# Compressed keys of all heads as one item of attention, and a round in the order transpositions, projection pieces, scores, values

## The reference

```python
def hybrid_mixer(h, cos, sin, w_in, cmp_pos, cmp_w1, cmp_w2, w_branch_nsa, w_branch_dil, w_out):
    q_n, kv_n, g_n, qkv_d, g_m = jnp.split(h @ w_in, cuts, axis=-1)
    ...
    kc = compress(kv_n[:, :, 0], cmp_pos[0], cmp_w1[0], cmp_w2[0])
    vc = compress(kv_n[:, :, 1], cmp_pos[1], cmp_w1[1], cmp_w2[1])
    ...
    y_nsa = nsa_attention(q_n, q_r, kc, vc, ks, kv_n[:, :, 3], kw, kv_n[:, :, 5], gates)
    ...
    y_dil = jnp.sum(alpha[..., None] * jnp.stack(outs, axis=2), axis=2).reshape(B, T, DIL_W)
    merged = g_m[:, :, 0] * (y_nsa @ w_branch_nsa) + g_m[:, :, 1] * (y_dil @ w_branch_dil)
    return merged @ w_out
```

## Time and profile before

| | |
|---|---|
| median of 3 runs | 1186.07 us (1183.7 to 1187.54) |
| the profiled execution | 1184.49 us |
| its span | 1182.7 us, mean TensorE clock 0.996 |
| busy, share of the span | TensorE 99%, VectorE 47%, ScalarE 34%, GpSimd 14% |
| the mixer | about 385 to 823 us |
| its attention stage | about 434 to 670 us |

### The profile page before, as it was taken

How to read it: one execution, slowest core, us unless ns; L and a number is a source line. 1 busy time by engine, 2 the same in 40 slices (tenths; PEclk the granted TensorE clock), 3 DMA queues, 4 the chain that set the end, 5 groups by cost and what they waited for, 6 DMA issues and landing times.

```text
span 1182.7 us, 16772 instructions
## 1 busy us (share of the span) xinstructions
PE 1170.4 (99%) x6707; PEld 956.4 (81%) x6707; DVE 561.5 (47%) x855; ACT 400.8 (34%) x532; POOL 170.3 (14%) x196
## 2 busy tenths in 40 slices
PE   9999999999999999999999999999999999999997
PEld 6888888888888987877777888888888888888886
DVE  6444344463333557567666444643544434432222
ACT  6323323232223225443535522233332332322222
POOL 1000000000112481356662000021000000000000
PEclk9999999999999999999999999999999999999998
DMA  7332333223336831412331233332333233223321
GB/s 228 107 105 75 104 106 90 76 73 99 97 97 153 189 81 46 95 46 43 79 79 31 73 98 89 107 107 71 107 106 105 76 103 106 82 77 98 98 74 71
DMA packets 211299, 110.85 MB, mean 94 GB/s; under 512 B 32112, under 2 KB 207648, under 8 KB 211248
## 3 DMA queue, kind: packets, MB, share of 16 engines
q1 hardware_dynamic: 206832, 104.97, 33.3%
q0 software_dynamic: 4256, 5.02, 1.7%
q10 hardware_dynamic: 160, 0.14, 0.0%
HBM read 105.06 MB, written 2.10 MB: 91 GB/s over the span
## 4 chain that ended last, share of the span: by engine, by line
PE 98%; DVE 1%; DMA 0%; SPq 0%; ACT 0%; issue 0%; DVEq 0%; ACTq 0%
PE ps L1300 23%; PE ps L1301 22%; PE ps L1302 22%; PE ps L1419 7%; PE ps L1418 7%; PE ps L1417 7%; PE ps L1558 2%; PE ps L1491 2%; PE ps L1535 2%; PE ps L1508 1%; PE ps L1574 1%; PE ps L1530 1%; DMA x_nat<-in_x 0%; PE ps L1478 0%; PE ps L1549 0%; PE ps L1524 0%
## 5 line engine op out<-in xcount | busy, mean ns | idle before, releaser
L930 DVE TENSOR_TENSOR w_lo<-w_raw,w_hi 128x2048 fp32r<-128x2048 f32 (+5 forms) x116 | 224.5, 1935 | 380.5 <-ACT w_hi L693 380.3
L1300 PE MATMUL ps<-xg_hi,w_hi 128*128 128x512 f32 x992 | 390.6, 394 | 0.4 <-DVE xg_lo L1212 0.4
L1302 PE MATMUL ps<-xg_hi,w_lo 128*128 128x512 f32 x992 | 386.4, 390 | 0.0
L1301 PE MATMUL ps<-xg_lo,w_hi 128*128 128x512 f32 x992 | 386.2, 389 | 0.0
L693 ACT ACTIVATE w_hi<-w_raw 128x2048 fp32r<-128x2048 f32 (+3 forms) x104 | 180.5, 1736 | 337.5 <-PE ps L1302 214.9
L1300 PEld LDWEIGHTS ps<-xg_hi,w_hi 128*128 128x128 f32 x992 | 186.2, 188 | 43.8 <-issue 6.2
L1302 PEld LDWEIGHTS ps<-xg_hi,w_lo 128*128 128x128 f32 x992 | 186.2, 188 | 39.2
L1301 PEld LDWEIGHTS ps<-xg_lo,w_hi 128*128 128x128 f32 x992 | 186.3, 188 | 37.2
L1417 PE MATMUL ps<-p_hi,w_hi 128*128 128x512 f32 x352 | 137.0, 389 | 0.0
L1419 PE MATMUL ps<-p_hi,w_lo 128*128 128x512 f32 x352 | 136.9, 389 | 0.0
L1418 PE MATMUL ps<-p_lo,w_hi 128*128 128x512 f32 x352 | 136.9, 389 | 0.0
(11 more groups left out here) (198 smaller groups left out, 1159.3 us busy)
## 6 DMA issues: line engine op xcount, KB each, us to landing
w_raw<-in_ffn_w_in SPq DMA_DIRECT2D x86, 512.0 KB, 5.0
w_raw<-in_w_in SPq DMA_DIRECT2D x32, 512.0 KB, 5.2
w_raw<-in_ffn_w_out SPq DMA_DIRECT2D x32, 384.0 KB, 3.6
w_raw<-in_ffn_w_out SPq DMA_DIRECT2D x32, 320.0 KB, 4.1
w_raw<-in_w_in SPq DMA_DIRECT2D x24, 256.0 KB, 4.6
w_raw<-in_w_out SPq DMA_DIRECT2D x8, 512.0 KB, 4.0
x_nat<-in_x SPq DMA_DIRECT2D x8, 256.0 KB, 4.9
w_raw<-in_w_branch_nsa SPq DMA_DIRECT2D x8, 256.0 KB, 4.1
```

The lines of the kernel that those rows point to most:

```text
L930: lo = V.tensor_tensor(w_lo[:, s, c], w_raw[:, s, c], w_hi[:, s, c].bitcast(F32), ALU.subtract)
L1300: mm(out, ah, bh, start=(first and i == 0), stop=False)
L1301: mm(out, ah, bl, start=False, stop=False)
L1302: last = mm(out, al, bh, start=False, stop=(final and i == len(pairs) - 1))
```

## The change

The item "cmp" is done once for all heads. The four heads' scores over 32 keys now stand side by side and fill the 128 columns of each query tile; softmax, transposition and copy are done on all of it. VectorE's and ScalarE's instructions of that item are four times as wide, TensorE transposes 8 blocks of 128 columns instead of 8 of 32 in each of four items, and the transposed probabilities go into a buffer of their own, `cmp_probs_t` (the tile `square`, free by then). The value products of head hh are issued at the head of its first "nsa" item (pe_cmp_values); for hh = 0 in the item's own place, at index 4 of the list. The compressed values are computed into four row groups for that. There are 25 NSA items and 41 in all, and 40 fills in rounds -1 to 38.

The scores, masks and exponentials of items 0 and 1 move ahead of the stage, before the first half of chunk 12 and before the second. The rounds change on all three engines.

```diff
         for hh in range(HPG):
-            ITEMS.append(("cmp", hh))
             ITEMS += [("nsa", hh, i, qts) for qts in ((0, 1), (2,), (3,)) for i in range(2)]
+        ITEMS.insert(4, ("cmp", 0))
...
-                                         ("hidden_t",), ("chunk", N_CH1, (0, KD // 2)), ("cmp_kv",),
-                                         ("chunk", N_CH1, (KD // 2, KD)), ("read_rest",), ("attend", 0, len(ITEMS))]
+                                         ("hidden_t",), ("scores", 0), ("chunk", N_CH1, (0, KD // 2)), ("cmp_kv",),
+                                         ("scores", 1), ("chunk", N_CH1, (KD // 2, KD)), ("read_rest",), ("attend", 0, len(ITEMS))]
...
         def act_attend(act, a, b):
-            act_exp(act, a)
-            act_exp(act, a + 1)
             for n in range(a, b):
                 act_copy_probs(act, n)
-                if n + 2 < b:
-                    act_exp(act, n + 2)
-                if n > a and ends_pair(n - 1) is not None:
-                    act_y(act, n - 1)
                 c = filled(n - 1)
                 if c is not None and ends_unit(c):
                     act_split(act, MIX0 + CH[c][1] + 2)
                 if splits_y(n) is not None:
                     act_split_y(act, splits_y(n))
+                if n + 2 < b:
+                    act_exp(act, n + 2)
+                if n > a and ends_pair(n - 1) is not None:
+                    act_y(act, n - 1)
...
                 if n + 1 < b:
                     dve_factor(dve, n + 1)
-                if n + 2 < b:
-                    dve_prepare(dve, n + 2)
-
                 for unit, half in SPLITS.get(n, ()):
                     dve_split(dve, MIX0 + unit, half=half)
                 if splits_y(n - 1) is not None:
                     dve_split_y(dve, splits_y(n - 1))
+                if n + 2 < b:
+                    dve_prepare(dve, n + 2)
...
             if it[0] == "cmp":
-                hh = it[1]
                 for g in range(2):
-                    mm(ps[:, b + g, :].rearrange("p (q k) -> p q k", q=TT)[:, :, 0:NC], ident_b,
-                       cmp_b.rearrange("p (q n) -> p q n", q=TT), start=True, stop=False)
+                    mm(ps[:, b + g, :].rearrange("p (q h n) -> p q h n", q=TT, h=HPG), ident_b,
+                       cmp_b.rearrange("p (q n) -> p q n", q=TT).unsqueeze(2).broadcast_to([P, TT, HPG, NC]),
+                       start=True, stop=False)
                 for qt in range(TT):
-                    for g in range(2):
-                        rows = slice(g * DH, g * DH + DH)
-                        last = mm(ps[:, b + g, qt * P:qt * P + NC], pool[rows, Q_RAW + hh, qt * P:qt * P + P],
-                                  k_cmp[rows, 0:NC], start=False, stop=(qt == TT - 1))
+                    for hh in range(HPG):
+                        for g in range(2):
+                            rows = slice(g * DH, g * DH + DH)
+                            at = qt * P + hh * NC
+                            last = mm(ps[:, b + g, at:at + NC], pool[rows, Q_RAW + hh, qt * P:qt * P + P],
+                                      k_cmp[rows, 0:NC], start=False, stop=(at == T - NC))
...
+        def pe_cmp_values(hh, opens):
+            rows = slice(hh * NC, hh * NC + NC)
+            for at, w in ((0, T),) if opens else ((0, 3 * P), (3 * P, P)):
+                for g in range(2):
+                    last = mm(ps[g * DH:g * DH + DH, 6, at:at + w], v_cmp[rows, g, :],
+                              cmp_probs_t[rows, g * T + at:g * T + at + w], start=opens, stop=False)
+            return last
...
         def pe_attend(pe, a, b):
-            pe_scores(pe, a)
-            pe_scores(pe, a + 1)
             pe_fill(pe, -1)
             for n in range(a, b):
                 pe_transpose_probs(pe, n)
+                if n in FILL:
+                    pe_fill(pe, n)
                 if n + 2 < b:
                     pe_scores(pe, n + 2)
-                late = n > a + 1 and ITEMS[n - 1][0] == "cmp"
-                if n > a and not late:
-                    pe_values(pe, n - 1)
-                if n in FILL:
-                    pe_fill(pe, n)
-                if late:
+                if n > a:
                     pe_values(pe, n - 1)
...
                     for g in range(2):
-                        last = mm(ps[0:NC, 7, g * DH:g * DH + DH], hid_t[:, 1, g * NC:g * NC + NC], w2[:, 1, :],
-                                  start=True, stop=True)
+                        for hh in range(HPG):
+                            last = mm(ps[hh * NC:hh * NC + NC, 7, g * DH:g * DH + DH], hid_t[:, 1, g * NC:g * NC + NC],
+                                      w2[:, 1, :], start=True, stop=True)
```

More of the change, by code:

```diff
@@ L338, in build @@
         for hh in range(HPG):
-            ITEMS.append(("cmp", hh))
             ITEMS += [("nsa", hh, i, qts) for qts in ((0, 1), (2,), (3,)) for i in range(2)]
+        ITEMS.insert(4, ("cmp", 0))
         N_NSA = len(ITEMS)
-        PER_HH = N_NSA // HPG
+        LAST_OF = [ITEMS.index(("nsa", hh, 1, (TT - 1,))) for hh in range(HPG)]
         for hp in range(2):
@@ L359, in ends_pair @@
             if n < N_NSA:
-                return n // PER_HH if n % PER_HH == PER_HH - 1 else None
+                return LAST_OF.index(n) if n in LAST_OF else None
             return 4 + (n - N_NSA) // 8 if (n - N_NSA) % 8 == 7 else None
@@ L466, in build @@
             and max(FILL) < len(ITEMS) - 1
-        assert all(max(fill_of(N_CH2 + 2 * hh)) >= PER_HH * (hh + 1) - 3 for hh in range(3))
+        assert all(max(fill_of(N_CH2 + 2 * hh)) >= LAST_OF[hh] - 2 for hh in range(3))
         SPLITS = {0: [(CH[C_Q + 3][1] + 2, 0)], 1: [(CH[C_Q + 3][1] + 2, 1)]}
@@ L879, in _ @@
                     nc.scalar.activation(hid[:, :], ps[:, 7, 0:P], ACT.Silu).then_inc(hid_ready, 1)
+                elif step[0] == "scores":
+                    act_exp(act, step[1])
                 elif step[0] == "attend":
@@ L1247, in _ @@
                     V.tensor_copy(k_cmp[:, 0:NC], ps[:, 7, 384:384 + NC])
-                    V.tensor_copy(v_cmp[:, :, :].rearrange("p a c -> p (a c)"), ps[0:NC, 7, 0:P]).then_inc(cmp_ready, 1)
+                    V.tensor_copy(v_cmp[:, :, :].rearrange("p a c -> p (a c)"), ps[:, 7, 0:P]).then_inc(cmp_ready, 1)
+                elif step[0] == "scores":
+                    dve_prepare(dve, step[1])
                 elif step[0] == "attend":
@@ L1543, in pe_values @@
             pe.wait_ge(pt_act, n + 1)
-            pair = n // PER_HH if n < N_NSA else 4 + (n - N_NSA) // 8
+            pair = it[1] if n < N_NSA else 4 + (n - N_NSA) // 8
             if pair:
@@ L1547, in pe_values @@
             if it[0] == "cmp":
-                for g in range(2):
-                    last = mm(ps[g * DH:g * DH + DH, 6, :], v_cmp[:, g, :], probs_t[0:NC, e, g * T:g * T + T],
-                              start=True, stop=False)
-                last.then_inc(pv_psum, 1)
+                pe_cmp_values(0, False).then_inc(pv_psum, 1)
                 return
@@ L1554, in pe_values @@
                 _, hh, i, qts = it
+                opens = i == 0 and qts[0] == 0
+                if opens and hh:
+                    pe_cmp_values(hh, True)
                 for qt, at, w in spans(qts):
@@ L1559, in pe_values @@
                                       probs_t[:, e, g * T + at + kt * P:g * T + at + kt * P + P],
-                                      start=False, stop=(i == 1 and kt == qt and qt == TT - 1))
+                                      start=(opens and hh == 0 and qt == 0), stop=(i == 1 and kt == qt and qt == TT - 1))
                 last.then_inc(pv_psum, 1)
```

54 lines of the change are left out of this document (29 added, 25 removed).

## The result

The changed kernel takes 1198.7 us (median of 4 runs, 1197.5 to 1201.1) against 1185.8: ratio 1.0105, 95% interval 1.0085 to 1.0124. The prediction was 1198. Two of the kernels further down had one run each of several times the usual length (2371 and 4142 us), which their medians leave out.

The account below looks back on a forecast made before the run. TensorE, busy nearly throughout the attention stage, was taken to bound the kernel. Terms -4.4 - 1.9 - 1.0 + 20.5 = +13.2 on 1184.49 us gave 1197.7, taken as 1198 from the runs' median; range 1189 to 1206.

Parts of the forecast that it names:

- The merge: TensorE's compressed items: one in place of four saves transpositions, scores, value shape changes and fill beginnings, less added copies; -4.4 us.
- The order itself: TensorE's rounds: transpositions are shorter before a fill than before scores, 0.05 us per round over 38 rounds; -1.9 us.
- The first wait: TensorE's first transposition, waiting for VectorE's scaled probabilities: earlier scores shrink 1.5 us to about 0.5; -1.0 us.
- GpSimd's hold: Rival: GpSimd's rope products lengthen VectorE's operations, now on the path, in up to half of 13 rounds; +6, 1204; chance 0.14.
- The fills' waits: TensorE's fills that begin a chunk wait for VectorE's evacuation, now behind masks that wait for scores; 17.9 us.
- the long ones: Rounds 2, 3, 17, 20 and 23, whose preceding fill is short: the fill waits 1.9 us each; +9.6 us.
- the gates: Dilated rounds 27, 30, 33, 36 beginning a gate chunk, only transpositions as cover: 1.2 three times, 0.8 once; +4.4 us.
- the plain rounds: Fills with values and transpositions as cover wait 0.1 to 0.7 us for evacuation; eleven fills, mean 0.35, +3.9 us.
- Waits elsewhere: TensorE waits 1.4 us at the last items, without fill cover, and 1.2 for probabilities elsewhere; +2.6 us.
- Sum: Whole kernel: -4.4 - 1.9 - 1.0 + 20.5 = +13.2 us on the profiled execution.
- The clock: Rival: TensorE's clock falls behind the new waits, one slow stretch after each of five long ones; +15, 1213; chance 0.04.

Follow-up runs that it names:

- later_rope: The merge_alone kernel with GpSimd's rope of the fourth query slot held back until the third item is scaled; 1179.0 us, ratio 0.9943.
- before_later: The kernel before the change, with only GpSimd's rope of the fourth query slot held back until the third item is scaled; 1182.9 us, ratio 0.9979.
- merge_alone: The changed kernel with the old round order on TensorE, VectorE and ScalarE, keeping the merged item and early scores; 1181.7 us, ratio 0.9950.
- Experiments 1 and 3: 1: merge_alone. 3: the changed kernel with VectorE's evacuation of a fill moved into that fill's round, at three places; 1183.2, 1186.45 and 1185.6 us.
- split_behind: The changed kernel with VectorE's weight splits put behind the masks again, evacuation left at the head of the next round; 1219.2 us, ratio 1.0286.
- order_alone: The kernel before the change with the new round order on three engines and nothing of the merge; 1208.0 us, ratio 1.0189.
- hybrid_later: The changed kernel with old order in dilated rounds, evacuations ahead of splits and masks in NSA rounds, rope held as in later_rope; 1180.5 us, ratio 0.9964.

## Why the prediction was right

- **The merge, -4.4.** later_rope's stage against before_later's, both without a wait and at a clock of 1.00: 653.3 - 657.4 = -4.2 (from unrounded values). Right.
- **The order itself, -1.9.** The changed kernel's stage less its waits, 672.3 - 19.7 - 1.0 - 0.3, is 651.4 (from unrounded values); later_rope, the same work in the old order without waits, has 653.3: -1.9. The steps show it as the prediction worked it out: transpositions are 0.12 us shorter ahead of a fill than ahead of scores (0.63, 0.85 and 0.41 against 0.75, 0.97 and 0.53 for 6, 8 and 4), and a fill is 0.07 longer ahead of scores (3.04 against 2.97). The rule of the Trainium skill ("TensorEngine Tiling (Array Packing)", Tiling Modes) would have made it 0, counting drains alone; by these steps, what a change costs depends on which kinds of product follow one another.
- **The first wait, -1.0.** 1.45 became 0.26. The size was right and the reason wrong. Earlier scores alone gave nothing (merge_alone: 1.50); the wait is GpSimd's hold, and in the changed kernel the first scalings happened to take 2.05 us, not 3.05. That this term came out is luck.
- **The fills' waits, 17.9.** 19.7 measured, the long ones and the gates to 0.1. Experiments 1 and 3 show the cause from both sides: the waits go when the three engines have the old order again, and when one call on VectorE is moved with TensorE's order left as it is. The missing 1.8 are in the plain rounds, of which 13 waited and not 11: 0.7 is round 13, where GpSimd's hold delays the masks, and the rest some tenths in each of several others.
- **Waits elsewhere, 2.6.** The mis-sized term: 1.0. Only the last pair of items waits for probabilities, and 1.0 instead of 1.4.
- **Sum.** -4.2 - 1.9 - 1.2 + 19.7 + 1.0 = +13.4, the 13.4 of the stage. Two terms missed by 1.6 to 1.8 us in opposite directions, so the time is closer than the working was. The span grew by 13.9: the profiled execution also began its feed-forward step 0.6 us later than before, which no term had.
- **The rivals.** GpSimd's hold is worth 1.1 us at the fills of the changed kernel, not 6. The clock did not fall in the stage in the profiled execution of the change. Where it fell behind a long wait (three times in split_behind, once in order_alone) it cost about 1.6 us in order_alone, not the 2.9 of a whole fill at half the clock; that the waits brought it about is likely and not shown, since it also fell where there was none. The Trainium skill ("TensorE: Matmul & The Clock Gate", Part 1) ties the fall to an idle engine; split_behind agrees with it, hybrid_later has 0.86 and 0.80 without any wait in the stage.

## What to carry to other kernels

When a producer's step is moved later in the round, look at the queue of the engine that frees its buffer: a ready evacuation that stands behind an operation with a wait inherits that wait, and one call moved on that engine (15.5 us here) can be worth more than the reordering it serves. Count a wait from start to start against the same step without one. And where a small operation of one engine takes several times its usual length, look for what runs beside it, and move that to where the delay has cover, not just later.

## What the runs showed of the hardware

- VectorE's TENSOR_SCALAR and TENSOR_TENSOR between SBUF tiles took longer while GpSimd's products ran: four scalings 3.05 us against 1.01, a split 2.31 against 1.22, an 8-column operation 1.15 against 0.17 (before, before_later). Not every operation did: a TENSOR_REDUCE of 256 columns took 0.41 us beside GpSimd in before and 0.41 without it in before_later. Masks and evacuations, which read PSUM, kept their length (512 columns: 0.67 to 0.73 in the stage of every trace read).
- Twenty-two waits of up to 2.0 us left the clock at 1.00 throughout the changed kernel's stage. Where 11 of the waits were of 1.7 to 2.4 us (split_behind), it fell to half in four stretches (at 461, 570, 618 and 648 us), 17 us in sum, and the time beyond the waits of fills was some 6 us.
- A block of 64 products of 32 columns can be followed by 3 to 4 us at half speed, without a wait: in merge_alone the products of the fill at 457.7 us come every 0.21 us, and every 0.12 from 460.4. The window there:

```profile
455.00:460.00 5.00, 5.00 (x53) 4.63 (x52) 2.63 (x3) 0.60 (x1) 0.00 (x0) 0.70 0.46 121
```
